# Held weight pieces half a 64-byte line into their slot, slots eight words longer, in a two-block float32 network

## The reference

```
h = h + 0.5 * swiglu(rmsnorm(h), ffn_w_in, ffn_w_out)      # ffn0: 1024 -> 2 x 2816 -> 1024
h = h + mlstm_mixer(rmsnorm(h), a_w_in, ..., a_w_out)
h = h + 0.5 * swiglu(...)                                  # ffn1
kv = nsa_shared_kv(h, kv_norm, kv_w, cmp_pe, cmp_w1, cmp_w2, k_norm)
h = h + 0.5 * swiglu(...)                                  # ffn2
h = h + nsa_mixer(rmsnorm(h), kv, b_w_in, b_q_norm, b_w_out)
h = h + 0.5 * swiglu(...)                                  # ffn3
x = layer_norm(ALPHA * x + fox_mixer(x))                   # q, k, v, forget gate, output gate
x = layer_norm(ALPHA * x + dsa_mixer(x))                   # attention over 64 chosen keys
```

## Time and profile before

| | us |
|---|---|
| three runs | 1310.18, 1311.35, 1311.47 |
| median | 1311.35 |
| span of the profiled execution, first to last instruction | 1310.3 |
| TensorE busy | 1270.2 (97%) |
| TensorE's weight loads busy | 1077.6 (82%) |
| VectorE busy | 873.9 (67%) |
| ScalarE busy | 613.6 (47%) |
| HBM read | 216.04 MB, 166 GB/s over the span |

### The profile page before, as it was taken

The page is one execution under the profiler, slowest core; times in us unless marked ns, Lnnn a source line. Parts: engine busy times, 40 slices in busy tenths (PEclk is TensorE's granted clock), DMA queues, the critical chain, the costliest instruction groups (busy, mean ns, idle before and its releaser), DMA issues.

```text
span 1310.3 us, 16491 instructions
## 1 busy us (share of the span) xinstructions
PE 1270.2 (97%) x6717; PEld 1077.6 (82%) x6717; DVE 873.9 (67%) x1312; ACT 613.6 (47%) x839; POOL 24.2 (2%) x37
## 2 busy tenths in 40 slices
PE   6999999989999999999999999999999999999997
PEld 5888888988788888878888886778888899988876
DVE  6655557885755556685657569856555567566896
ACT  6444346435434445444435357654444344544461
POOL 2000000100000000000000000000000000000000
PEclk9999999999999999999999989999999999999999
DMA  9655545443555556565665440065666686446401
GB/s 329 207 182 187 186 162 185 142 155 129 183 184 185 188 192 186 166 193 170 217 224 169 159 161 1 1 200 187 191 193 193 130 217 172 150 130 211 176 2 65
DMA packets 158812, 218.17 MB, mean 167 GB/s; under 512 B 8257, under 2 KB 110993, under 8 KB 158737
## 3 DMA queue, kind: packets, MB, share of 16 engines
q1 hardware_dynamic: 156880, 212.56, 51.2%
q0 software_dynamic: 1376, 3.71, 0.9%
q10 hardware_dynamic: 480, 0.85, 0.2%
HBM read 216.04 MB, written 1.05 MB: 166 GB/s over the span
## 4 chain that ended last, share of the span: by engine, by line
PE 82%; DVE 11%; issue 3%; ACT 2%; SPq 1%; DMA 1%; DVEq 0%
PE PS L686 23%; PE PS L689 23%; PE PS L687 23%; DVE wlo L2050 2%; PE PS L823 1%; PE PS L721 1%; PE PS L722 1%; ACT whi L1523 1%; PE PS L706 1%; PE PS L1300 1%; DVE arena L2639 1%; PE PS L728 1%; PE PS L1016 1%; SPq L591 1%; DVE XL L2090 1%
## 5 line engine op out<-in xcount | busy, mean ns | idle before, releaser
L2050 DVE TENSOR_TENSOR wlo<-raw,whi 128x2048 fp32r<-128x2048 f32 (+4 forms) x206 | 457.4, 2230 | 122.6 <-ACT whi L1523 121.8
L1523 ACT ACTIVATE whi<-raw 128x2048 fp32r<-128x2048 f32 (+4 forms) x206 | 381.4, 1863 | 63.4 <-DMA raw<-in_fox_w_in_dram 33.1
L686 PE MATMUL PS<-whi,XL 128*128 128x512 f32 (+3 forms) x992 | 385.8, 390 | 8.9 <-DVE scr L2152 3.8
L687 PE MATMUL PS<-wlo,XH 128*128 128x512 f32 (+3 forms) x992 | 379.8, 384 | 0.0
L689 PE MATMUL PS<-whi,XH 128*128 128x512 f32 (+3 forms) x992 | 265.0, 384 | 0.0
L686 PEld LDWEIGHTS PS<-whi,XL 128*128 128x128 f32 x992 | 187.3, 189 | 45.1 <-DVE scr L2152 4.9
L689 PEld LDWEIGHTS PS<-whi,XH 128*128 128x128 f32 x992 | 185.5, 190 | 35.5
L687 PEld LDWEIGHTS PS<-wlo,XH 128*128 128x128 f32 x992 | 187.4, 189 | 32.9
L1577 ACT ACTIVATE scr<-PS,rn 128x256 f32<-128x256 f32 x88 | 41.7, 474 | 225.2 <-PE PS L689 223.9
L686 PE MATMUL PS<-whi,GL 128*128 128x512 f32 x320 | 125.4, 392 | 0.0
L687 PE MATMUL PS<-wlo,GH 128*128 128x512 f32 x320 | 124.6, 389 | 0.0
(11 more groups left out here) (387 smaller groups left out, 1339.2 us busy)
## 6 DMA issues: line engine op xcount, KB each, us to landing
raw<-in_ffn_w_in_dram SPq DMA_DIRECT2D x174, 512.0 KB, 5.0
raw<-in_ffn_w_out_dram SPq DMA_DIRECT2D x88, 512.0 KB, 4.9
raw<-in_fox_w_in_dram SPq DMA_DIRECT2D x24, 512.0 KB, 7.9
raw<-in_a_w_in_dram SPq DMA_DIRECT2D x16, 512.0 KB, 4.6
raw<-in_dsa_w_in_dram SPq DMA_DIRECT2D x16, 512.0 KB, 6.0
raw<-in_kv_w_dram SPq DMA_DIRECT2D x12, 512.0 KB, 4.2
raw<-in_fox_w_in_dram SPq DMA_DIRECT2D x12, 344.0 KB, 5.0
raw<-in_a_w_out_dram SPq DMA_DIRECT2D x8, 512.0 KB, 4.9
```

Of the source, the lines that this page charges most:

```text
L686: mm(o, xl, wh, start=start and i == 0, stop=False, skip_group_check=True)
L687: mm(o, xh, wl, start=False, stop=False, skip_group_check=True)
L1523: A(whi[:, p % SLOTS, 0:n], raw[:, p % SLOTS, 0:n], ACT.Copy).then_inc(hi_done, 1)
L2050: V.tensor_tensor(wlo[:, p % SLOTS, 0:n], raw[:, p % SLOTS, 0:n], whi[:, p % SLOTS, 0:n].bitcast(F32), ALU.subtract).then_inc(lo_done, 1)
```

## The change

All instructions stay, in the same order with the same waits on every engine; only places in SBUF change.

- A slot is 2,056 words (8,224 bytes) in `whi`, `wlo` and `raw`, so that every second slot begins half a line off. Eight unused words behind `whi` and `wlo` bring what follows back to a multiple of 64.
- `begins` marks the pieces of B chunks. `held(buf, p, n)` gives the place of a piece in its slot: a marked piece begins eight words into an even slot and at the start of an odd one, which is half a line off in both; every other piece begins at the start of an even slot and eight words into an odd one, which is on a line in both. All loads, copies, subtractions and matmuls use it.
- Relative to a multiple of 256 bytes, the pieces that are not marked began all at one place; now they begin 0, 64, 64, 128, 128, 192 and 192 bytes further in slots 0 to 6.
- To make room, the arena is 112 words shorter: the NSA gates `n_gt` and the first part of the DSA selection `d_sel` move into `GL`, the rest of `d_sel` behind `d_wuv`, and `f_gate` by 64 words. All keep their place in the line.

```diff
+SLOT = PIECE + 8
...
+    begins = {}
+    for name, (_, chunks) in stages.items():
+        p = first_piece[name]
+        for kind, _, n in chunks:
+            for _ in range(2 if n * KT > PIECE else 1):
+                if kind == B_CHUNK:
+                    begins[p] = 8
+                p += 1
...
-        whi = sb("whi", [P, SLOTS, PIECE], F32R)
+        whi = sb("whi", [P, SLOTS, SLOT], F32R)
+        sb("half_line", [P, 8])
         lo_at = (nc.sbuf_base + 31) // 32 * 32
-        wlo = sb("wlo", [P, SLOTS, PIECE], F32R)
-        raw = nc.alloc_sbuf_tensor_at("raw", [P, SLOTS, PIECE], F32, offset=lo_at)
+        wlo = sb("wlo", [P, SLOTS, SLOT], F32R)
+        raw = nc.alloc_sbuf_tensor_at("raw", [P, SLOTS, SLOT], F32, offset=lo_at)
+
+        def held(buf, p, n=PIECE):
+
+            at = begins.get(p, 0)
+            at = 8 - at if p % SLOTS % 2 else at
+            return buf[:, p % SLOTS, at:at + n]
+
+        sb("half_line_2", [P, 8])
...
+        d_sel0 = nc.alloc_sbuf_tensor_at("d_sel0", [P, P], F32, offset=gl_at + 4 * 384)
+        n_gates = nc.alloc_sbuf_tensor_at("n_gates", [P, 96], F32, offset=gl_at)
...
-        AW = 12672
+        AW = 12560
...
-        n_qT, n_gt, n_cs, n_cpT = carve(keep, 2048, 96, 1024, 1024)
+        n_qT, n_cs, n_cpT = carve(keep, 2048, 1024, 1024)
...
-        f_qT, f_kT, f_v, f_gate, d_sel = carve(0, 2048, 2048, 2048, 2048, 384)
+        f_qT, f_kT, f_v, _, f_gate = carve(0, 2048, 2048, 2048, 64, 2048)
...
-                        dst = raw[:, p % SLOTS, 0:n].rearrange("p (k n) -> p k n", k=k)
+                        dst = held(raw, p, n).rearrange("p (k n) -> p k n", k=k)
...
             def parts_n(p, k, n):
-                return (whi[:, p % SLOTS, 0:k * n].rearrange("p (k n) -> p k n", k=k),
-                        wlo[:, p % SLOTS, 0:k * n].rearrange("p (k n) -> p k n", k=k))
+                return (held(whi, p, k * n).rearrange("p (k n) -> p k n", k=k),
+                        held(wlo, p, k * n).rearrange("p (k n) -> p k n", k=k))
...
-                A(whi[:, p % SLOTS, 0:n], raw[:, p % SLOTS, 0:n], ACT.Copy).then_inc(hi_done, 1)
+                A(held(whi, p, n), held(raw, p, n), ACT.Copy).then_inc(hi_done, 1)
...
-                V.tensor_tensor(wlo[:, p % SLOTS, 0:n], raw[:, p % SLOTS, 0:n], whi[:, p % SLOTS, 0:n].bitcast(F32),
+                V.tensor_tensor(held(wlo, p, n), held(raw, p, n), held(whi, p, n).bitcast(F32),
                                 ALU.subtract).then_inc(lo_done, 1)
```

More of the change, by code:

```diff
@@ L260, in program @@
         t_PT = t_PT.rearrange("p (b s j t) -> p b s j t", b=2, s=2, j=4)
-        n_qT, n_gt, n_cs, n_cpT = carve(keep, 2048, 96, 1024, 1024)
+        n_qT, n_cs, n_cpT = carve(keep, 2048, 1024, 1024)
         n_qT = n_qT.rearrange("p (k t) -> p k t", k=KT)
-        n_gt = n_gt.rearrange("p (t c) -> p t c", t=NT)
+        n_gt = n_gates[:, :].rearrange("p (t c) -> p t c", t=NT)
         n_cs = n_cs.rearrange("p (t h n) -> p t h n", t=NT, h=QH)
         n_cpT = n_cpT.rearrange("p (t g q) -> p t g q", t=NT, g=KVH)
-        f_qT, f_kT, f_v, f_gate, d_sel = carve(0, 2048, 2048, 2048, 2048, 384)
+        f_qT, f_kT, f_v, _, f_gate = carve(0, 2048, 2048, 2048, 64, 2048)
         f_qT = f_qT.rearrange("p (k t) -> p k t", k=KT)
@@ L279, in program @@
         d_kT = d_kT.rearrange("p (k t) -> p k t", k=KT)
-        d_ckr, d_ckvT, d_krT, d_wuv = carve(4096, 320, 256, 256, 1024)
+        d_ckr, d_ckvT, d_krT, d_wuv, d_sel1 = carve(4096, 320, 256, 256, 1024, 256)
         d_ckr = d_ckr.rearrange("p (t c) -> p t c", t=NT)
@@ L583, in load_in @@
                         free_slot(p)
-                        dst = raw[:, p % SLOTS, :].rearrange("p (k w n) -> p k w n", k=4, w=2)
+                        dst = held(raw, p).rearrange("p (k w n) -> p k w n", k=4, w=2)
                         if p == 0:
@@ L596, in load_out @@
                     free_slot(p)
-                    dst = raw[:, p % SLOTS, :].rearrange("p (k n) -> p k n", k=2)
+                    dst = held(raw, p).rearrange("p (k n) -> p k n", k=2)
                     for w in range(2):
@@ L605, in load_cmp @@
                         free_slot(p)
-                        dst = raw[:, p % SLOTS, :].rearrange("p (k n) -> p k n", k=8)
+                        dst = held(raw, p).rearrange("p (k n) -> p k n", k=8)
                         src = rows(a["cmp_w1"][kv], 8 * half, 8, 0, 256)
@@ L692, in parts @@
             def parts(p, k):
-                return (whi[:, p % SLOTS, :].rearrange("p (k n) -> p k n", k=k),
-                        wlo[:, p % SLOTS, :].rearrange("p (k n) -> p k n", k=k))
+                return (held(whi, p).rearrange("p (k n) -> p k n", k=k),
+                        held(wlo, p).rearrange("p (k n) -> p k n", k=k))
             def turn_h(name, t, w):
@@ L2881, in choose @@
                 cols = slice(0, P) if t == 0 else slice(P, 384)
-                work, isc, sel_ = d_work[:, cols], d_isc[:, cols], d_sel[:, cols]
+                work, isc, sel_ = d_work[:, cols], d_isc[:, cols], d_sel0[:, :] if t == 0 else d_sel1
                 cm = caus[:, P:2 * P] if t == 0 else caus
@@ L2916, in d_mask @@
             def d_mask(t, g, j):
-                return d_sel[:, 0:P] if t == 0 else d_sel[:, P:384]
+                return d_sel0[:, :] if t == 0 else d_sel1
             split_to(first + 12)
```

## The result

The changed kernel takes 1324.81 us (median of 4 runs, 1323.76 to 1326.96), against 1311.41 us for the kernel before on the same chip (4 runs). The ratio is 1.01, with a 95% interval from 1.0082 to 1.0118: slower by about 13 us. The forecast was 1309.1 us with a range up to 1312.3. It was wrong, and by more than any rival on record.

The account below looks back on a forecast made before the run. TensorE's matmuls were taken to bound the kernel (busy 97% of 1310.3 us). The held pieces' 2.2 us on the path, all else 0, gave a span of 1308.1, plus 1.05 around it: 1309.1 us, range 1305.6 to 1312.3.

Parts of the forecast that it names:

- Step 3: Streamed pieces, slots 8,224 bytes apart: taken as 0, bounds 0.8 ns on 6/7 of 3,984 matmuls, 2.7 us either way.
- the streamed pieces pay: Rival: shifted slots make the FFNs' matmuls 0.8 ns slower, net 0.5 us worse than before, 1311.9 us; chance 0.15.
- Step 1: B chunks: 960 matmuls with held pieces half a line off go from 120.0 to 116.7 ns, 3.2 us of TensorE's time.
- Step 2: Gain on the path: 576 matmuls in fox and 96 in mLSTM count, DSA's none; 672 times 3.3 ns, 2.2 us.
- Steps 4 to 6: ScalarE's copies and VectorE's subtractions of held pieces, loads (bounds plus and minus 0.3 us), moved tensors: each taken as 0.

Follow-up runs that it names:

- experiment 2: Matmul streams appended to the kernel before, streamed or held operand moved by varying bytes; at 512 columns 226.7 ns unmoved, 232.9 with the streamed one moved 192 bytes.
- Experiment 1: Changed kernel with no held piece displaced: 1325.16 us; kernel before with 64 or 32 unused bytes ahead of `h`: 1332.56 and 1332.39 us.
- experiment 3: Changed kernel with slots at 2,048 words: nothing displaced 1314.06 us, fox's 12 held pieces 32 bytes down 1313.37, 192 down 1313.99; kernel before 1312.82.
- experiment 4: Slots of 2,048 words, kernel before 1311.6 us: extra load wait alone 1314.25; 11 fox pieces 32 or 192 bytes down without that wait 1310.23, 1309.95.
- The kernel with its slots back: Changed kernel with slots at 2,048 words, no held piece displaced, moved tensors kept: 1314.06 us, ratio 1.0002 against the kernel before.

## Why the prediction was wrong

**Step 3 failed, the streamed pieces, taken at 0 with a bound of 0.8 ns each.** They cost 3.9 ns each, 15.5 us, nearly six times the bound of 2.7 us. The step rested on the earlier trace rows: 344 columns with pieces at eight places of 256 bytes, 157.5 ns where the line through the two clean widths gave 156.7. The inference was that a place off the multiple costs next to nothing. It mixes two things. The pieces of 344 columns cycle through eight distances even inside one piece, so a row of twelve is a mean, with no row of 344 columns at distance 0 to compare it to. And the effect of a distance depends on the width: at 192 bytes 512 columns lose 6 ns, 384 columns 1.9, and 256 columns gain (experiment 2). Nothing in the trace of before had 512 columns at any other distance than 0: the trace had no row from which to bound it, and that is a reason for a wide bound, not for the nearest row. The 372-column rows, 1.7 ns above the line and set aside because their place in the 64 bytes differed, pointed the right way; what one fixed distance costs at that width was not measured.

The rival "the streamed pieces pay" named the place and the sign of what happened. It had the size wrong by a factor of five (0.8 ns), or of two by the 372-column rows (1.7), and it argued against itself with "their place in the 64 bytes is kept". Experiment 1 shows that this keeps nothing: 64 bytes cost as much as 32.

**Step 1, the held pieces, 3.3 ns.** The size was right for one distance and wrong for the change. The compressions of the earlier trace rows were 116.7 ns since their operands lay 32 bytes apart modulo 256; moved to that distance and no other, fox's B chunks gain 3.1 ns (experiment 3). But the changed kernel lays its held pieces at four distances, among them 96, where the row at 234.90 still has 120.0. From fox's first B matmul to the scores behind 480 of them it takes 59.44 us, 0.80 less than the 60.24 of a kernel at distance 0 (experiment 3), 1.7 ns on each:

```profile
1084.03 0.28 PE L706 MATMUL PS<-XH,wlo 128*128 128x256 f32 x1
...
1143.47 2.82 PE L1416 MATMUL PS<-arena 128*128 128x128 f32 x19
```

The prediction saw a confound in its pair of rows, which "differs in the name of the passing operand too". It was neither that name nor the half line as such: it was the 32 bytes between the two operands.

**Step 2, what of it is on the path.** Held for fox: in the kernels without the pitch the gain of the stretch is still there at the last matmul (experiment 4). For 672 matmuls it would be 1.7 x 672 = 1.1 us in the changed kernel. With 15.5 that gives a loss of 14.4 us, where the medians are 13.4 us apart. The trace, too, loses 14.4 us from 31 us on, but 1.5 of them are the clock, so the equality is luck. The 1.5 us between 14.4 and 12.9 lie at least in part in waits for VectorE that became shorter: the one ahead of the small matmuls of the mLSTM stage is 1.03 us before and 0.68 after.

**Steps 4 to 6.** These held as far as the runs can tell. VectorE's and ScalarE's busy times differ by 0.1 and 0.5 us; ScalarE waits 32.4 us for fox's landings, 33.1 before. The kernel with its slots back has all the moved tensors and stands at 1.0002.

**The weighing of the Trainium skill.** "TensorE: Matmul & The Clock Gate", section "Step-by-step: what each phase is for", has the next weight load take no read bandwidth from the running matmul. Here a stream gets slower by up to 3% when only the place of the held operand, which is what the load reads, is moved (the rows from 1434.87 on). The rows give distances from start to start, so they cannot say whether the running matmul is slowed or the next one starts later; either way the place of the load's operand is not free. The same page's section "Back-to-back issue gap" says that the formula which the prediction took from it is for a single matmul, that it comes out too low at small widths in a stream with weight loads, and gives about 131 ns at 512 columns for such a stream. The first part agrees in direction: 120.0 ns here against the formula's 109.2 at 256 columns, so the prediction was wrong that the page lacks this. The 131 ns do not agree with any row here: 512 columns take 226.7 ns at distance 0 and up to 234.6 at others. The measurement decides. Why the distance matters, and why its sign turns at 256 columns, no run here shows.

## What to carry to other kernels

Before changing the pitch or the base of a buffer that matmuls read, write down the places of both operands modulo 256 bytes for each form. A difference that is the same in thousands of matmuls, as the zero here, may be what the kernel's speed rests on, and any unused tensor allocated in between can lose it (21 us of 1311 here). A bound for an operation at a place where the trace has none is not given by a row of another width; put the form itself at that place in a short stream and measure it. And when pieces share space, ask which load must now wait for one piece more: 1.5 us gained in the matmuls was paid back behind one late landing.

## What the runs showed of the hardware that was not expected

- The pace of a float32r matmul with a weight load each time depends on the difference of the two operands' places modulo 256 bytes: for 512 columns 226.7 ns at 0, 230 to 235 at the other places of the scan (240 is still as good as 0: 227.1); for 256 columns 120 at 0, and at 192 either 113 to 114 or 117.8, which of the two is not explained.
- Moving both operands alike changes nothing (227.1 ns), and moving one by 256 or 512 bytes changes nothing (227.9 and 227.1).
- How much a distance costs depends on the width: at 192 bytes 6 ns of 227 at 512 columns, 1.9 of 173.5 at 384. Rows of 344 columns, which run through eight distances, took 157.5 ns before and 156.7 after; what one fixed distance costs there was not measured.
